# A first projection streamed by modulation pair, host-laid activations and four in-place weight slots in a two-layer diffusion trunk

## The chip, the core and the metric

The kernel runs on one core of one Trainium2 chip. The core has TensorE (PE, matmuls), VectorE (DVE), ScalarE (ACT), GpSimd (POOL) and SyncE (SP, which here only issues DMAs). Each engine works through its own list of instructions in order and meets the others only at semaphores. The metric is the device time of one execution in microseconds (us), the median of several. Where a profile is read, its own execution has a time too, and both are given.

## What is computed

A denoising step of a trunk with two layers, for 128 context and 256 latent tokens of width 1024, all in float32. Cut to what matters here:

```python
def modulate(x, g, shift, scale):
    return rms_norm(x, g) * (1 + scale) + shift
def swiglu(h, w_in, w_out):                      # w_in 1024 x 5632, w_out 2816 x 1024
    gate, up = jnp.split(h @ w_in, 2, axis=-1)
    return (jax.nn.silu(gate) * up) @ w_out
def macaron_layer(x, mod, norm_g, ffn_in, ffn_out, mixer):
    m = mod[:, :, None, :]                       # mod = silu(cond) @ w_mod + b_mod, 9 vectors of 1024
    x = x + 0.5 * m[:, 2] * swiglu(modulate(x, norm_g[0], m[:, 0], m[:, 1]), ffn_in[0], ffn_out[0])
    mixed, own_kv = mixer(modulate(x, norm_g[1], m[:, 3], m[:, 4]))
    x = x + m[:, 5] * mixed
    x = x + 0.5 * m[:, 8] * swiglu(modulate(x, norm_g[2], m[:, 6], m[:, 7]), ffn_in[1], ffn_out[1])
```

Layer 0 mixes with attention and a convolution, layer 1 with a Fourier transform and a gated unit. Context and latent tokens have conditioning vectors of their own (`c_ctx`, `c`). The outputs are the tokens of both groups, and keys and values of the context.

## The kernel before

**Stages.** Six sub-layers run one after the other, numbered s: FFN 0, the even mixer (1), FFN 2, FFN 3, the odd mixer (4), FFN 5. Tokens lie in the free dimension (384 columns: 128 context, 256 latent), channels in the partitions, eight blocks d of 128 channels. Ahead of each sub-layer stands a norm: ACT squares x, POOL and PE sum the squares, ACT and DVE make the reciprocal root, PE spreads it over the partitions, and DVE and ACT scale and shift x, block by block.

**Units.** All projection weights come in 153 units of 1 MiB (128 partitions x 2048). Every product is done by three matmuls on rounded parts: ACT copies the raw weights to `w_hi` (L528), DVE subtracts to get `w_lo` (L790), and PE computes high*high, high*low and low*high (L1185 to L1187): 48 matmuls of 384 columns a unit. An FFN has 33 units: 22 of w_in (units 0 to 21, one step each: ACT silu L557, DVE product L895, ACT `h_hi` L559, DVE `h_lo` L898), then 11 of w_out (22 to 32, the out phase). Raw, high and low parts have rings of three slots (RING = 3), and SP loads unit u as soon as the low part of unit u-3 is made (`lo_done`).

**Modulation.** Nine vectors for each of two layers are 144 row tiles of 128 outputs. The first 18 are computed at the start on PE from nine 1 MiB blocks (`w_pairs`; L1231 sums, L797 copies them out, L1241 turns them to columns). The other 126 are row tiles of 0.5 MiB (`w_rows`): for each, DVE multiplies the tile by the two conditioning rows (two L812 products, each with a sum along the row). They have a ring of three buffers: SP loads tile n after tile n-3 is used (`tile_used`). Tables say how many go with what: `TILES_BEFORE`, `TILE_LOOPS` (one tile with every step of an FFN's loop) and `TILES_OUT` (how many with each unit of the out phase). The next norm needs some of them.

**Order around the change.** In FFN s, step t of DVE splits unit t+2, makes product t and `h_lo` t, then works off its tiles. In the out phase DVE splits unit 24+j and then works off `TILES_OUT[s][j]` tiles. SP issues in one list: in the loop unit t+2, then the tile of step t; in the out phase unit 24+j, then the tiles of j. An SP instruction that waits holds all that stand behind it.

**The start.** PE transposes the conditioning rows (L1341) and x (L1350), DVE copies x out of PSUM (L947), ACT issues 13 small DMAs of vectors (L522), which PE transposes too. When all 18 tiles are done, the norm's last step runs, and FFN 0 begins with unit 0. Two conditioning rows are then loaded, and ACT applies silu (L589). **The end.** After the last residual (L852) PE transposes x back (L1573), ACT copies (L773), and SP stores (L436).

Of the kernel before, what the change touches and what calls it, by code (L numbers as in the profile page):

```python
# [26 lines left out]
P = 128  # L27
# [19 lines left out]
N_SUB = 6  # L47
# [6 lines left out]
RING = 3  # L54
MRING = 3
UNIT = 2048
# [14 lines left out]
GROUPS_FIRST = 3  # L71
LOOPS = (FT - 1) // RING
FIRST_TILES = MRING * GROUPS_FIRST * PAIR_TILES
MOD_TILES = 2 * MODT - FIRST_TILES
TILES_BEFORE = {0: 3, 2: 0, 3: 0, 5: 2}
TILE_LOOPS = {0: LOOPS, 2: LOOPS, 3: LOOPS, 5: 2}
TILES_OUT = {0: [3, 3] + [2] * 8, 2: [2] + [1] * 9, 3: [3] + [2] * 8 + [0], 5: [0] * 10}
TILE0, _t = {}, 0
for _s in (0, 2, 3, 5):
    TILE0[_s] = _t  # L80
    _t += TILES_BEFORE[_s] + MRING * TILE_LOOPS[_s] + sum(TILES_OUT[_s])
assert _t == MOD_TILES and MRING == RING
# [3 lines left out]
COND_AT = 2 * (MRING - 1)  # L86
# [70 lines left out]
def modulation_pairs(w_mod):  # L157

    n = MRING * GROUPS_FIRST
    w = w_mod[0, :, 0:n * PAIR].reshape(KT, P, n, PAIR).transpose(2, 1, 0, 3)  # L160
    return np.ascontiguousarray(w, dtype=np.float32).reshape(n, P, UNIT)
# [8 lines left out]
def build(nc, x_prompt, x_sample, cache_k, cache_v, c, c_ctx, b_mod, norm_g,  # L170
          q_norm_g, k_norm_g, conv_w, conv_b, conv_norm_g, conv_norm_b,
          sgu_norm_g, sgu_norm_b, sgu_w, sgu_b, k_ident, k_rope, k_fourier, w_units, w_pairs, w_rows,
          y_prompt, y_sample, new_cache_k, new_cache_v):
    ctx = ExitStack()
    with ctx:
# [99 lines left out]
        cols_copied = sem("cols_copied")  # L275
        const_in, cond_in, x_in = sem("const_in"), sem("cond_in"), sem("x_in")
        cond_t = sem("cond_t")
# [3 lines left out]
        rows_t, rows_c = sem("rows_t"), sem("rows_c")  # L281
        cond_ready = sem("cond_ready")
        x_t = sem("x_t")
# [9 lines left out]
        out_in, out_t, out_c, out_done = sem("out_in"), sem("out_t"), sem("out_c"), sem("out_done")  # L293
# [38 lines left out]
        def mod_rows(b):  # L332
            return m_raw[:, b, 0:D_MODEL]

        def cond_row(cnd):
            return m_raw[:, cnd, D_MODEL:UNIT]

        def row_products():
            return m_raw[:, 2, D_MODEL:UNIT]
# [3 lines left out]
        def _(sp):  # L343
            def load_unit(u, i=0):

                sp.wait_ge(lo_done, u + 1 + RING * i)
                sp.dma_start(w_raw[:, slot(u), :].unsqueeze(1),
                             w_units[bass.ds(u + i * RING, 1)].rearrange("u p n -> p u n")).then_inc(raw_in[slot(u)], 16)

            def load_pair(group, b, i=0):  # L350

                sp.wait_ge(mod_used, MRING * group + b + 1 + MRING * i)
                sp.dma_start(m_raw[:, b, :].unsqueeze(1),
                             w_pairs[bass.ds(MRING * group + b + i * MRING, 1)].rearrange("u p n -> p u n")
                             ).then_inc(mod_in[b], 16)

            def load_tile(n, i=0):

                if n >= MRING:
                    sp.wait_ge(tile_used, n - MRING + 1 + MRING * i)  # L360
                sp.dma_start(mod_rows(n % MRING).unsqueeze(1),
                             w_rows[bass.ds(n + MRING * i, 1)].rearrange("t p n -> p t n")).then_inc(tile_in[n % MRING], 16)

            def load_ffn(s):
                u0, n = UNIT0[s], TILE0[s]

                if s == 0:
# [24 lines left out]
                n += MRING * TILE_LOOPS[s]  # L392
# [1229 lines left out]
```

## Time and profile before

| what | us |
|---|---|
| median of three runs | 1502.31 (1501.9 to 1505.26) |
| the profiled execution | 1499.5 |
| its span, first to last instruction | 1497.7 |
| TensorE busy in it | 1407.8 (94%) |
| VectorE busy | 970.0 (65%) |
| mean granted TensorE clock | 0.964 |

The span is the time from the profile's first to its last instruction; 1.8 us lie around it. Busy time of PE is that of pipelined matmuls, with modelled ends. "Idle before" is the time in which an engine had nothing to do ahead of an instruction, with the work that ended it. Times of day below are from the span's start.

### The profile page before, as it was taken

The numbers are of one execution on the slowest core, as the hardware profiler recorded it, in microseconds if no ns is written. First come the engines' busy times: TensorE is split into PE (matmuls) and PEld (weight loads), VectorE is DVE, ScalarE is ACT, GpSimd is POOL, SyncE is SP. The second block draws the span as 40 slices with busy tenths as digits, with TensorE's granted clock in tenths as the row PEclk, the third lists the DMA queues.
The fourth block names the chain that finished last, engine by engine and source line by source line (L and its number), as shares of the span: only waits on it lengthen the run. The fifth ranks groups of instructions, "written<-read, shape, count | busy, mean of one in ns | idle before, by whom it ended". The sixth has DMA issues, their size and how long they took to land.

```text
span 1497.7 us, 21193 instructions
## 1 busy us (share of the span) xinstructions
PE 1407.8 (94%) x8134; PEld 1375.4 (92%) x8134; DVE 970.0 (65%) x1394; ACT 557.7 (37%) x731; POOL 122.5 (8%) x110
## 2 busy tenths in 40 slices
PE   5799999989866899999998999999989989999998
PEld 3799999989845799999998999999989989999998
DVE  2777678968998566666757666679763477444332
ACT  2433332237666443333224333332345343333221
POOL 1000000014555100000001000000021010000000
PEclk9899999989878999999998999999989999999999
DMA  8765655752200235555652555547523325433421
GB/s 325 261 231 176 203 177 200 285 182 96 86 32 29 102 133 201 188 191 174 234 181 85 197 193 185 193 149 295 219 99 134 126 85 186 137 122 130 141 84 42
DMA packets 45114, 242.96 MB, mean 162 GB/s; under 512 B 4997, under 2 KB 6889, under 8 KB 24328
## 3 DMA queue, kind: packets, MB, share of 16 engines
q1 hardware_dynamic: 44464, 241.99, 46.7%
q8 instruction: 32, 0.52, 0.1%
q10 hardware_dynamic: 600, 0.30, 0.1%
q14 instruction: 18, 0.15, 0.0%
HBM read 240.57 MB, written 1.70 MB: 162 GB/s over the span
## 4 chain that ended last, share of the span: by engine, by line
PE 83%; DVE 10%; DMA 2%; ACT 2%; issue 1%; POOL 1%; ACTq 0%; SPq 0%; DVEq 0%; POOLq 0%
PE ps L1185 27%; PE ps L1186 27%; PE ps L1187 27%; DVE conv L974 4%; DVE w_lo L790 1%; DMA conv_rows<-in_conv_w 1%; DVE n_full L876 1%; PE ps L1254 1%; DVE m_raw L812 1%; DVE smax L1039 1%; ACT w_hi L528 1%; DVE a_lo L883 0%; POOL n_acc L453 0%; DMA m_raw<-in_w_pairs 0%; PE ps L1554 0%
## 5 line engine op out<-in xcount | busy, mean ns | idle before, releaser
L1185 PE MATMUL ps<-a_hi,w_hi 128*128 128x384 f32 x1744 | 591.7, 339 | 19.1 <-DVE a_lo L883 14.0
L1186 PE MATMUL ps<-a_lo,w_hi 128*128 128x384 f32 x1744 | 588.5, 337 | 0.0
L1187 PE MATMUL ps<-a_hi,w_lo 128*128 128x384 f32 x1744 | 588.1, 337 | 0.0
L790 DVE TENSOR_TENSOR w_lo<-w_raw,w_hi 128x2048 fp32r<-128x2048 f32 x153 | 352.9, 2306 | 162.3 <-ACT w_hi L528 162.0
L528 ACT ACTIVATE w_hi<-w_raw 128x2048 fp32r<-128x2048 f32 x153 | 292.1, 1909 | 264.7 <-PE ps L1187 200.2
L1185 PEld LDWEIGHTS ps<-a_hi,w_hi 128*128 128x128 f32 x1744 | 332.1, 190 | 23.4 <-issue 10.0
L1186 PEld LDWEIGHTS ps<-a_lo,w_hi 128*128 128x128 f32 x1744 | 332.1, 190 | 0.1
L1187 PEld LDWEIGHTS ps<-a_hi,w_lo 128*128 128x128 f32 x1744 | 331.7, 190 | 0.0
L812 DVE SCALAR_TENSOR_TENSOR m_raw<-m_raw 128x1024 f32<-128x1024 f32 x252 | 296.0, 1220 | 1.0 <-ACT m_raw L589 1.0
L1187 PE MATMUL ps<-h_hi,w_lo 128*128 (+1 forms) x704 | 236.6, 336 | 0.0
L1186 PE MATMUL ps<-h_lo,w_hi 128*128 (+1 forms) x704 | 236.6, 336 | 0.0
L1185 PE MATMUL ps<-h_hi,w_hi 128*128 (+1 forms) x704 | 236.6, 336 | 0.0
L557 ACT ACTIVATE glu<-ps 128x384 f32<-128x384 f32 x88 | 43.4, 493 | 376.6 <-PE ps L1187 376.6
L895 DVE TENSOR_TENSOR glu<-glu,ps 128x384 f32<-128x384 f32 x88 | 48.7, 554 | 167.2 <-ACT glu L557 167.2
L1187 PEld LDWEIGHTS ps<-h_hi,w_lo 128*128 128x128 f32 x704 | 132.4, 188 | 0.0
L1185 PEld LDWEIGHTS ps<-h_hi,w_hi 128*128 128x128 f32 x704 | 132.4, 188 | 0.0
L1186 PEld LDWEIGHTS ps<-h_lo,w_hi 128*128 128x128 f32 x704 | 132.4, 188 | 0.0
L898 DVE TENSOR_TENSOR h_lo<-glu,h_hi 128x384 f32 (+1 forms) x88 | 49.2, 559 | 71.6 <-ACT h_hi L559 71.6
L453 POOL TENSOR_TENSOR n_acc<-n_sq 128x384 f32<-128x384 f32 x6 | 6.1, 1014 | 973.4 <-ACT n_sq L538 879.5
L559 ACT ACTIVATE h_hi<-glu 128x384 f32 (+1 forms) x88 | 46.2, 525 | 86.4 <-DVE glu L895 86.4
L473 POOL TENSOR_TENSOR conv<-conv,taps_buf 128x399 f32<-128x399 f32 x60 | 72.9, 1215 | 51.5 <-ACT taps_buf L618 45.6
L974 DVE SCALAR_TENSOR_TENSOR conv<-padded,conv_wt,conv 128x399 f32<-128x399 f32 x60 | 61.1, 1018 | 1.6
(179 smaller groups left out, 666.2 us busy)
## 6 DMA issues: line engine op xcount, KB each, us to landing
w_raw<-in_w_units SPq DMA_DIRECT2D x153, 1024.0 KB, 5.0
m_raw<-in_w_rows SPq DMA_DIRECT2D x126, 512.0 KB, 3.6
m_raw<-in_w_pairs SPq DMA_DIRECT2D x9, 1024.0 KB, 7.7
out<-x_nat SPq DMA_DIRECT2D x3, 512.0 KB, 3.1
x_nat<-in_x_sample SPq DMA_DIRECT2D x1, 1024.0 KB, 12.5
fourier<-in_k_fourier SPq DMA_DIRECT2D x1, 768.0 KB, 4.4
x_nat<-in_x_prompt SPq DMA_DIRECT2D x1, 512.0 KB, 10.7
m_raw<-in_c_ctx SPq DMA_DIRECT2D x1, 512.0 KB, 5.7
```

Of the source, the lines that this page charges most:

```text
L473: nc.gpsimd.tensor_tensor(acc, acc, taps_buf[:, n % TAP_BUFS, :], ALU.add).then_inc(tap_added, 1)
L528: nc.scalar.activation(w_hi[:, slot(u), :], w_raw[:, slot(u), :], ACT.Copy).then_inc(hi_done, 1)
L557: nc.scalar.activation(glu[:, 0, :], ps[:, 2 * b, 0:TOK], ACT.Silu).then_inc(silu_done, 1)
L559: nc.scalar.activation(h_hi[:, bass.ds(t + RING * i, 1), :], glu[:], ACT.Copy).then_inc(h_hi_done, 1)
L790: nc.vector.tensor_tensor(w_lo[:, slot(u), :], w_raw[:, slot(u), :], w_hi[:, slot(u), :].bitcast(FP32), ALU.subtract).then_inc(lo_done, 1)
L812: nc.vector.scalar_tensor_tensor(out, mod_rows(n % MRING), 1.0, cond_row(cnd), ALU.mult, ALU.mult, accum_out=mod_cols[:, bass.ds(FIRST_TIL ...
L895: nc.vector.tensor_tensor(glu[:, 0, :], glu[:, 0, :], ps[:, 2 * b + 1, 0:TOK], ALU.mult).then_inc(prod_done, 1)
L898: nc.vector.tensor_tensor(h_lo[:, bass.ds(t + RING * i, 1), :], glu[:], h_hi[:, bass.ds(t + RING * i, 1), :].bitcast(FP32), ALU.subtract). ...
L974: ins = nc.vector.scalar_tensor_tensor(conv[:, j, :], padded[:, j, k:k + CONV_N], conv_wt[:, j, k:k + 1], conv[:, j, :], ALU.mult, ALU.add)
L1185: mm(out, whi, mhi, start=start, stop=False)
L1186: mm(out, whi, mlo, start=False, stop=False)
L1187: return mm(out, wlo, mhi, start=False, stop=stop)
```

## The change

Four things, made together:

1. **The start.** The host lays out x, the conditioning vectors, all small vectors and the result in the kernel's own layout; the transposes, the copies and the 13 small DMAs go. FFN 0's first shift and scale (16 tiles) come in eight blocks, block k holding shift and scale of channel block k, all with a buffer of their own (`p_raw`). Units 0 and 1 are multiplied in k order as the pairs arrive. All squares of the first norm are summed on PE (none on POOL).
2. **The end.** Each block of x is stored after its residual, without transposes.
3. **Weight slots.** RING = 4; `w_raw` and `w_lo` share memory, so that DVE subtracts in place, and SP loads unit u only when PE is done with unit u-4 (`unit_done`).
4. **Tiles.** 128 tiles are left; the loop of an FFN has five rounds of four steps with 1, 2, 1, 2 tiles, still with three buffers, and `TILES_OUT` changes. The loop of SP loads units 3 to 22 where it loaded units 3 to 23.

```diff
-RING = 3
+RING = 4
 MRING = 3
+TRING = 3
+STEP_TILES = [1, 2, 1, 2]
-LOOPS = (FT - 1) // RING
-FIRST_TILES = MRING * GROUPS_FIRST * PAIR_TILES
+LOOPS = (FT - 2) // RING
+FIRST_TILES = KT * PAIR_TILES
-TILES_OUT = {0: [3, 3] + [2] * 8, 2: [2] + [1] * 9, 3: [3] + [2] * 8 + [0], 5: [0] * 10}
+TILES_OUT = {0: [2] * 7 + [1, 0, 0], 2: [1, 1] + [0] * 8, 3: [2] * 5 + [0] * 5, 5: [0] * 10}
...
             def load_unit(u, i=0):
-                sp.wait_ge(lo_done, u + 1 + RING * i)
+                sp.wait_ge(unit_done, u + 1 + RING * i)
...
                                 load_unit(u0 + 3 + RING * done + b, i)
                                 if with_tiles:
-                                    load_tile(n + b, i)
+                                    for t in range(STEP_TILES[b]):
+                                        load_tile(n + sum(STEP_TILES[:b]) + t, i)
...
                 for j, tiles in enumerate(TILES_OUT[s]):
-                    if j < FFN_OUT_UNITS - 2:
-                        load_unit(u0 + FT + 2 + j)
+                    load_unit(u0 + FT + 1 + j)
                     for _ in range(tiles):
                         load_tile(n)
                         n += 1
...
+            mod_sums(0)
             mod_columns(0)
+            for d in range(KT):
+                pe.wait_ge(sq_done, d + 1)
+                ins = token_sums(ps[:, 0, :], n_sq[:, d, :], d, d == KT - 1)
+            ins.then_inc(stat_done, 1)
             norm_spread(0)
+            mod_sums(1)
             mod_columns(1)
+            for k in range(KT):
+                if k + 2 < KT:
+                    mod_sums(k + 2)
+                pe.wait_ge(a_ready, k + 1)
+                for m in range(2):
+                    if k == 0:
+                        pe.wait_ge(lo_done, RING + m + 1)
+                    for h in range(2):
+                        ins = three(ps[:, 2 * m + h, 0:TOK], tile_of(w_hi, m, h * KT + k), tile_of(w_lo, m, h * KT + k),
+                                    a_hi[:, k, :], a_lo[:, k, :], k == 0, k == KT - 1)
+                    if k == KT - 1:
+                        ins.then_inc(unit_done, 1)
+                if k + 2 < KT:
+                    mod_columns(k + 2)
...
+            for d in range(KT):
+                sp.wait_ge(x_ready, KT * N_SUB + d + 1)
+                sp.dma_start(y_cols[:, d, :], x[:, d, :]).then_inc(out_done, 16)
```

On DVE the first three tiles of FFN 0, which stood ahead of step 0, now stand after step 1:

```diff
+                step(0, 0, 0, [])
                 if s == 0:
                     dve.wait_ge(silu_rows, 2)
-                for _ in range(TILES_BEFORE[s]):
-                    mod_tile(n)
-                    n += 1
-                step(0, 0, 0, None)
+                step(1, 1, 0, range(n, n + TILES_BEFORE[s]))
```

SP at the change from the loop to the out phase of FFN 0, before; the first rows are the loop's last step (unit 23, a tile), then come unit 24, three tiles, unit 25, and so on:

```order
L347 ISA [waits lo_done]
L347 DMA w_raw<-in_w_units 128x2048
L361 ISA [waits tile_used]
L361 DMA m_raw<-in_w_rows 128x1024
L386 REGISTER_ALU
L386 COMPARE_AND_BRANCH
L347 DMA w_raw<-in_w_units 128x2048 [waits lo_done]
L361 DMA m_raw<-in_w_rows 128x1024 [waits tile_used] x3
L347 DMA w_raw<-in_w_units 128x2048 [waits lo_done]
L361 DMA m_raw<-in_w_rows 128x1024 [waits tile_used] x3
```

And now; the loop's last step is unit 22 and two tiles, and the next units are 23, 24 and so on:

```order
L350 ISA [waits unit_done]
L350 DMA w_raw<-in_w_units 128x2048
L360 ISA [waits tile_used]
L360 DMA m_raw<-in_w_rows 128x1024
L360 ISA [waits tile_used]
L360 DMA m_raw<-in_w_rows 128x1024
L389 REGISTER_ALU
L389 COMPARE_AND_BRANCH
L350 DMA w_raw<-in_w_units 128x2048 [waits unit_done]
L360 DMA m_raw<-in_w_rows 128x1024 [waits tile_used] x2
L350 DMA w_raw<-in_w_units 128x2048 [waits unit_done]
L360 DMA m_raw<-in_w_rows 128x1024 [waits tile_used] x2
```

Each unit stands one step later against the tiles: the tiles of j stood behind unit 24+j, now they stand ahead of it.

PE at the start, before, from the sums of the first norm on (`n_sq`, `n_acc` are squares, `rows` small vectors):

```order
L1247 MATMUL ps<-ones,n_sq 128x1 [waits sq_done,x_ready]
L1247 MATMUL ps<-ones,n_sq 128x1 x2
L1247 MATMUL ps<-ones,n_sq 128x1 [waits sq_done]
L1247 MATMUL ps<-ones,n_sq 128x1 x2
L1247 MATMUL ps<-ones,n_acc 128x1 [waits acc_done]
L1247 MATMUL ps<-ones,n_acc 128x1 x2
```

And now, the last block's sums and what follows up to the first product of the projection:

```order
L1238 MATMUL ps<-ones,n_sq 128x1 [waits sq_done]
L1238 MATMUL ps<-ones,n_sq 128x1 x2
L1245 MATMUL ps<-n_diag,ones 128x128 [waits diag_done]
L1245 MATMUL ps<-n_diag,ones 128x128 x2
L1222 MATMUL ps<-m_raw,cond 32x256 [waits pair_in1]
L1222 MATMUL ps<-m_raw,cond 32x256 x7
L1232 MATMUL ps<-mod_pick,mod_part 128x2 [waits first_mods,part_copied]
L1232 MATMUL ps<-mod_pick,mod_part 128x2
L1222 MATMUL ps<-m_raw,cond 32x256 [waits part_copied,pair_in2]
L1222 MATMUL ps<-m_raw,cond 32x256 x7
L1175 MATMUL ps<-a_hi,w_hi 128x384 [waits lo_done,a_ready]
```

The sums stand in eight groups of three where there were three (each shows as six matmuls in the trace, in two passes), and a pair's sums stand between the products.

## Rows read from the trace of the kernel before

**Rows 1.** The page: busy time, share, instructions; then shares of the chain.

```profile
PE 1407.8 (94%) x8134; PEld 1375.4 (92%) x8134; DVE 970.0 (65%) x1394; ACT 557.7 (37%) x731; POOL 122.5 (8%) x110
PE 83%; DVE 10%; DMA 2%; ACT 2%; issue 1%; POOL 1%; ACTq 0%; SPq 0%; DVEq 0%; POOLq 0%
```

**Rows 2.** FFN 3: length, busy PE, PEld, DVE, ACT, POOL; clock, DMA share, GB/s.

```profile
811.10:1089.00 277.90, 277.55 (x1587) 277.23 (x1587) 201.57 (x280) 94.65 (x99) 4.06 (x4) 0.99 0.55 194
```

**Rows 3.** Timeline of PE, the start: start, duration, instruction, [idle before <-releaser].

```profile
7.56 1.93 PE L1231 MATMUL ps<-m_raw,cond 128*32 128x256 f32 x16 [4.03 <-DMA m_raw<-in_w_pairs]
10.05 1.93 PE L1231 MATMUL ps<-m_raw,cond 128*32 128x256 f32 x16 [0.56 <-DMA m_raw<-in_w_pairs]
...
22.90 1.50 PE L1247 MATMUL ps<-ones,n_sq 128*128 128x1 f32 x12
...
33.09 1.07 PE L1231 MATMUL ps<-m_raw,cond 128*32 128x256 f32 x16
...
41.53 1.02 PE L1241 MATMUL ps<-mod_pick,mod_part 128*128 128x6 f32 x4 [0.55 <-DVE mod_part L797]
...
67.53 0.45 PE L1185 MATMUL ps<-a_hi,w_hi 128*128 128x384 f32 x1 [1.60 <-DVE w_lo L790]
```

**Rows 4.** Timeline of PE around the norm after FFN 0.

```profile
325.39 0.34 PE L1187 MATMUL ps<-h_hi,w_lo 128*128 128x384 f32 x1
328.04 2.51 PE L1247 MATMUL ps<-ones,n_sq 128*128 128x1 f32 x12 [2.31 <-ACT n_sq L538]
...
335.24 1.65 PE L1254 MATMUL ps<-n_diag,ones 128*128 128x128 f32 x6 [1.29 <-DVE n_diag L865]
339.03 0.69 PE L1185 MATMUL ps<-a_hi,w_hi 128*128 128x384 f32 x1 [2.14 <-DVE a_lo L883]
```

**Rows 5.** Timeline of PE around the norm after FFN 2.

```profile
801.41 0.34 PE L1187 MATMUL ps<-h_hi,w_lo 128*128 128x384 f32 x1
...
811.10 0.66 PE L1185 MATMUL ps<-a_hi,w_hi 128*128 128x384 f32 x1 [2.23 <-DVE a_lo L883]
```

**Rows 6.** Timeline of DVE, two units of FFN 3's out phase.

```profile
1040.43 2.29 DVE L790 TENSOR_TENSOR w_lo<-w_raw,w_hi 128x2048 fp32r<-128x2048 f32 x1 [1.44 <-ACT w_hi L528]
1042.64 1.22 DVE L812 SCALAR_TENSOR_TENSOR m_raw<-m_raw 128x1024 f32<-128x1024 f32 x1
...
1048.75 2.29 DVE L790 TENSOR_TENSOR w_lo<-w_raw,w_hi 128x2048 fp32r<-128x2048 f32 x1 [1.45 <-ACT w_hi L528]
```

**Rows 7.** Timeline of SP there: start and duration of a unit's DMA issue.

```profile
1045.41 0.43 SPq L347 DMA_DIRECT2D w_raw<-in_w_units  x1
```

**Rows 8.** Timeline of ACT there.

```profile
1046.80 1.92 ACT L528 ACTIVATE w_hi<-w_raw 128x2048 fp32r<-128x2048 f32 x1 [6.40 <-PE ps L1187]
```

**Rows 9.** L347, issue to landing of the three units issued in 1036 to 1060.

```profile
DMA to landing us min/median/max: 5.7/5.8/5.8
```

**Rows 10.** L347, the same of the two units issued in 1008 to 1016.

```profile
DMA to landing us min/median/max: 6.6/6.8/7.0
```

**Rows 11.** Timeline of DVE, step 0 of FFN 0.

```profile
65.19 2.29 DVE L790 TENSOR_TENSOR w_lo<-w_raw,w_hi 128x2048 fp32r<-128x2048 f32 x1
67.40 0.55 DVE L895 TENSOR_TENSOR glu<-glu,ps 128x384 f32<-128x384 f32 x1
68.53 0.56 DVE L898 TENSOR_TENSOR h_lo<-glu,h_hi 128x384 fp32r<-128x384 f32 x1 [0.59 <-ACT h_hi L559]
```

**Rows 12.** Timeline of ACT ahead of it: a table load, the two conditioning rows.

```profile
54.98 1.28 ACT L589 ACT_TABLE_LOAD   x1
56.27 2.01 ACT L589 ACTIVATE m_raw<-m_raw 128x1024 f32<-128x1024 f32 x2
```

**Rows 13.** Timeline of DVE, the last residual.

```profile
1489.11 0.74 DVE L852 SCALAR_TENSOR_TENSOR x<-ps,m_gate,x 128x128 f32<-128x128 f32 x2 [0.30 <-PE ps L1187]
```

**Rows 14.** DMAs issued in the first 2 us: KB each, median us to landing.

```profile
m_raw<-in_w_pairs SPq DMA_DIRECT2D x1, 1024.0 KB, 5.5
ident<-in_k_ident SPq DMA_DIRECT2D x1, 64.0 KB, 1.9
```

More of the change, by code:

```diff
@@ L540, in norm_stats, with norm @@
                 nc.scalar.activation(stat[:, 4:4 + TT], stat[:, 0:TT], ACT.Sqrt).then_inc(root_done, 1)
-            def norm(n):
-                for d in range(KT):
+            def norm(n, d0=0, d1=KT):
+                for d in range(d0, d1):
                     for cnd, lo, hi in SEGS:
@@ L577, in _ @@
             norm_stats(0)
-            for v in range(2):
-                act.wait_ge(rows_t, v + 1)
-                nc.scalar.activation((vec_a, vec_b)[v][:], ps[:, 1 + v, 0:(A_ROWS, B_ROWS)[v]], ACT.Copy).then_inc(rows_c, 1)
-            act.wait_ge(rows_t, 3)
-            nc.scalar.activation(conv_wt[:], ps[:, 3, 0:CT * CONV_K].rearrange("p (a b) -> p a b", a=CT),
-                                 ACT.Copy).then_inc(rows_c, 1)
             split(0)
-            norm(0)
+            norm(0, 0, 1)
             split(1)
+            norm(0, 1, KT)
+            split(2)
             act.wait_ge(rows_in, 32)
@@ L770, in _ @@
             ffn(5)
-            for tt in range(TT):
-                act.wait_ge(out_t, tt + 1)
-                nc.scalar.activation(x_nat[:, tt, :].rearrange("p (a b) -> p a b", a=2), ps[:, 2 * tt:2 * tt + 2, :],
-                                     ACT.Copy).then_inc(out_c, 1)
         @block.vector
@@ L900, in step @@
                                             ALU.subtract).then_inc(h_ready, 1)
-                    if tile is not None:
+                    for tile in tiles:
                         mod_tile(tile, i)
+                step(0, 0, 0, [])
                 if s == 0:
                     dve.wait_ge(silu_rows, 2)
-                for _ in range(TILES_BEFORE[s]):
-                    mod_tile(n)
-                    n += 1
-                step(0, 0, 0, None)
+                step(1, 1, 0, range(n, n + TILES_BEFORE[s]))
+                n += TILES_BEFORE[s]
                 done = 0
@@ L990, in _ @@
             glu_mul(0)
[L991 removed]
+            dve.wait_ge(vectors_in, 48)
             split(u + 3)
@@ L1279, in step @@
                     in_unit(u0 + t, 2 * (t % RING), i)
-                first_units(u0, (0, 2), s, s != 0)
-                with pe.Fori(0, LOOPS - 1) as i:
+                if s:
+                    first_units(u0, (0, 2), s)
+                with pe.Fori(0, LOOPS) as i:
                     for b in range(RING):
                         step(2 + b, i)
-                for t in range(2 + RING * (LOOPS - 1), FT):
-                    step(t, 0)
                 def out_unit(u, t, i, first=False):
@@ L1293, in out_unit @@
                         mhi, mlo = h_hi[:, fm, :], h_lo[:, fm, :]
-                        for d in (2, 3, 4, 5, 6, 7, 0, 1) if first else range(KT):
-                            if first and h == 0 and d in (2, 4, 0):
-                                pe.wait_ge(prod_done, RING + FT * f + FT - {2: 2, 4: 1, 0: 0}[d])
+                        for d in (4, 5, 6, 7, 0, 1, 2, 3) if first else range(KT):
+                            if first and h == 0 and d % 2 == 0:
+                                pe.wait_ge(prod_done, RING + FT * f + FT - {4: 3, 6: 2, 0: 1, 2: 0}[d])
                             ins = three(ps[:, d:d + 1, 0:TOK], tile_of(w_hi, u, h * KT + d), tile_of(w_lo, u, h * KT + d),
@@ L1303, in ffn @@
                 pe.wait_ge(h_ready, 1 + FT * (f + 1))
-                with pe.Fori(0, (FFN_OUT_UNITS - 2) // RING) as i:
+                rounds = (FFN_OUT_UNITS - 2) // RING
+                with pe.Fori(0, rounds) as i:
                     for b in range(RING):
                         out_unit(u0 + FT + 1 + b, 1 + b, i)
+                for t in range(1 + RING * rounds, FFN_OUT_UNITS - 1):
+                    out_unit(u0 + FT + t, t, 0)
                 u = u0 + FFN_UNITS - 1
```

340 lines of the change are left out of this document (153 added, 187 removed).

## The prediction

> **What bounds the kernel now.** First the page, for which engine sets the end: TensorE (PE) is busy 94% of the span and carries 83% of the chain of waits, DVE 10% [rows 1]. Then busy time by stretch, to see where it is not PE: inside an FFN it is never anything else, 277.55 of 277.90 us in FFN 3 while DVE works 201.57 [rows 2]. So a gain can only come from the places where PE stands: the start, where unit 2 of FFN 0 begins at 67.53 [rows 3], the norms, and the end. In an FFN the change can only leave PE where it is or make it wait, and what decides that is how early SP may issue a load. Third, therefore, the timelines of DVE, SP and ACT in an out phase [rows 6 to 9].
>
> I keep one scale: the profiled execution of 1499.5 us, and add 2.8 at the end, by which the median is longer.
>
> **The out phase, where most of it is decided.** Call S the moment at which DVE starts a split. In FFN 3 S = 1040.43, the next split starts at 1048.75, which is PE's pace: 8.32 us a unit [rows 6]. A split takes 2.21 until the next instruction starts (1042.64), a tile is two products, 2.3 together. At 1045.41, S + 4.98, SP issues a unit [rows 7]: it had stood behind a tile that waits for the first tile of this unit's pair to be used. It lands 5.75 us later [rows 9], ACT makes its high part in 1.92, and DVE's split can follow 1.95 after ACT starts (1046.80 to 1048.75) [rows 6, 8]. So from S to the split of a unit whose load was held in this way are 4.98 + 5.75 + 1.95 = 12.7 us. Before, that was the split after the next, with 16.64 us of room. The change moves each unit one step back against the tiles: SP's list is now unit 23+j, two tiles, unit 24+j, and DVE wants 24+j in its step j. The second tile of step j waits, with three buffers, for the first tile of step j-1, and unit 24+j waits behind it. The 12.7 us now lie between one split and the next: as long as a step has two tiles behind two tiles, a unit takes **12.7 us instead of 8.32**, 4.4 lost each. PE runs two units behind the splits, but that lead is eaten before the rounds begin, as follows.
>
> FFN 3, with P the end of unit 21: product 21 comes at about P + 3.5 (PE wants it at P + 3.1, 18 matmuls into unit 22, each 8.32 / 48 = 0.173: 0.4 lost); `h_lo` and the first tile end near P + 6.9; unit 24 issued, landed and split 10.4 later, at P + 17.3, where PE wants it at P + 17.05: 0.2. Units 25 to 28 each come 12.7 after the one ahead: 4 x 4.4 = 17.6. Then the tiles are over. **FFN 3: +18.2.** FFN 2 has one tile with the first two units only, which wait for older tiles: only the 0.4 of product 21, **+0.4**. FFN 5 has none.
>
> **The start.** The first MiB lands 5.5 us after an issue at 1.9 [rows 14], the next 2.6 later (PE follows each landing [rows 3]). x (1.5 MiB) goes first: 8.7; pair 0 at 11.3. PE's sums over it take 1.93 at 1.2 GHz, the copy about 0.5 (the idle time ahead of the columns), the columns 1.02 [rows 3]: 14.8. Then the squares: 48 matmuls instead of 18 on PE. Twelve take 1.50 at the high clock [rows 3] and 2.51 at the low one [rows 4]. Which holds? Before, the sums over the first three pairs all took 1.93, and the clock rose only with the transposes of x, which go now. I take the low one: 4 x 2.51 = 10.0, to 24.8. Root and diagonal 1.3 (idle ahead of the spread), spread 1.65 [rows 4]; beside it ACT and DVE split unit 0 one after the other, 1.9 + 2.2, to 29.5. Scaling, shift and low part of block 0 follow (2.14 from spread to product before [rows 4], about 1.7 without block 1 in between), copy and columns of pair 1 (1.5), two small ones (0.3), split 1 (2.2): 35.3. PE does its first twelve products at the low clock (about 0.32 each, near double), until 38.5; columns 0.8; then five rounds at the high clock, sums 1.07 [rows 3], twelve products 2.08 and columns half of 1.02, 3.66 each: 18.3. Call the end of the last columns T: 58, half a microsecond for low clock in it. The pairs, 2.6 us apart, are ahead of this all the way. Unit 2 is split by ACT and DVE only after block 7 is scaled, T + 5.9: PE starts it at 63.9, against 67.53. **Start: -3.6.** A gain of twenty, which the stream looks like, is not in these rows: the serial chain, not the loads, is what is left.
>
> **FFN 0.** ACT loads a table and does the two rows first (3.3 [rows 12]); DVE's steps 0 and 1 (3.9 each from split to `h_lo` [rows 11]) end at T + 14.1, and only then come the three tiles. The load of unit 4 stands behind the tile that waits for the first of them: T + 16.4, issued 0.85 later, landed 5.6 later (the tile goes 0.6 ahead, not 0.4 as in [rows 9]), split 4.2 later: T + 27.1, where PE wants it at T + 22.5: **4.5**. From here DVE, SP and ACT turn in a loop of two steps: used tile, 0.85, 5.6, 1.95, then a step with two tiles (3.9 + 4.6) = 16.9 against PE's 16.64. DVE therefore never catches up; product 21 comes **5.1** after PE wants it. `h_lo` 21 and unit 24 cost 0.3 more. Units 25 to 30 cost 4.4 each: **26.4**. Together **+36.3**, a unit 32 that ends at 358 and not at 325.7.
>
> **Norm 1.** From the last product of FFN 0 to the first of the mixer PE took 13.64 us [rows 4], after FFN 2 9.69 [rows 5]; in the first case DVE was late from tiles that lay at the very end. Now the last units have none: **-4.0**.
>
> **The end.** The last residual ends at 1489.85 [rows 13], the span at 1497.7. Transposes, copies and the 512 KB stores go; a store of 192 KB is issued in 0.4 and lands within about 2.1, nearest to the 64 KB's 1.9 [rows 14]: 1492.4. **-5.3**, at worst -4.5 (a landing of 3).
>
> **Slots.** Splitting in place moves the same bytes. Loads now wait for PE's unit u-4, three units (25 us) ahead of need, against 9.9 for landing and split: no wait, also in the mixers. The extra rows of x, squares and small vectors on POOL and ACT are off the path.
>
> **Sum.** -3.6 + 36.3 - 4.0 + 0.4 + 18.2 - 5.3 = +42.0: 1541.5 on the profile's scale, **1544.3** for the median, 2.8% slower.
>
> **Rivals.** *The clock rises during the squares.* PE is busy without a break for 10 us there. Then squares and what follows go at the high clock: 4 us less in the squares, about 4 in columns, sums and first products, and all later times move up: 1536. Against it: the row of 1.93 us although PE was busy most of the time [rows 3]. For it: nothing in the rows has squares alone for so long. The Trainium skill, TensorE: Matmul & The Clock Gate, "What's actually happening", says that the throttled state is the default and activity releases it; by that rule this is the case that comes. The three 1.93 us sums before do not agree, the later rise with the transposes does. I give it 0.18.
>
> *Loads land late.* Where DVE worked without a pause, units took 6.6 to 7.0 us instead of 5.75 [rows 10]. Ten rounds at 1 us more, and eight double steps of FFN 0 at about as much, give +18: 1562. DVE is busy half of a 12.7 us round, so this is likelier in FFN 0's loop than in the rounds: 0.15.
>
> *The hold does not bite.* If the room at the start of the out phases were two splits instead of none, or SP's list ran ahead of what I read, nothing of the 54 us in the FFNs would come, and only the gains stay: 1499.5 - 3.6 - 4.0 - 5.3 + 2.8 = 1489.4, faster. It is decided by whether a round is over or under 8.32 us; landing alone is 5.75, split 4.2, so it would take an issue ahead of DVE's split. 0.07. A part of it (one FFN only, or half of the rounds), 1505 to 1530: 0.05.
>
> **How the numbers follow.** The forecast has 0.55; its own bounds (0.3 us a round, 3 in the start, 1 at the end) make 1538 to 1552. With the clock case below (1536, with the same bounds 1530) and late loads above it (to 1564) the range 1530 to 1564 leaves out the two faster ones and a few per cent above. A difference of 0.2%, 3 us, is about what a measurement of this kernel can tell from none. Faster 0.07, within it 0.01, slower 0.92.
>
> **What would show it.** In the profile after: in FFN 0's and FFN 3's out phases the splits 12.7 us apart, six and four times, PE waiting for the low part 4 us or so each time, and SP's unit issues 5 us after a split starts. Unit 4 of FFN 0 late by 4 to 5; unit 2 started near 64; twelve squares in 2.5 us. FFN 2 and 5 at 277 and 276 as before; norm 1 down to 9.7; the last store within 3 us of the last residual. Wrong it would be if splits in the out phases stay 8.32 apart, or if the mixers' units wait for their loads.

## The result, and the profile after

The changed kernel takes **1568.53 us** (median of four, 1561.49 to 1574.65), the kernel before in the same job 1502.29. The ratio is **1.0435 (95% interval 1.0384 to 1.0486)**: 66 us slower. Slower was forecast, at 1544.3 with a range up to 1564; the time lies above the range. The profiled execution took 1565.28, its span is 1563.5.

The page, answering [rows 1]: busy time, the chain, the costliest lines of the chain, and one group of the matmuls of the out phases.

```profile
PE 1436.2 (92%) x8113; PEld 1397.0 (89%) x8113; DVE 971.7 (62%) x1410; ACT 555.1 (36%) x725; POOL 113.6 (7%) x105
PE 46%; DVE 17%; DMA 16%; issue 11%; ACT 8%; SPq 1%; DVEq 1%; POOL 0%; ACTq 0%; POOLq 0%
...
L1175 PE MATMUL ps<-h_hi,w_hi 128*128 (+1 forms) x704 | 245.1, 348 | 49.1 <-DVE w_lo L767 33.3
```

PE carried 83% of the chain and now carries 46%; loads, DVE and ACT have taken its place. PE is also busy 28 us longer with fewer matmuls; 23 of them lie in FFN 0 and FFN 3, with as many matmuls as before and a lower granted clock (rows below). What it waited for (total, times, longest; `w_lo` is a unit's low part, `glu` a product):

```profile
PE ps L1175 <- DVE w_lo L767: 39.2, 14, 7.2
PE ps L1175 <- DVE glu L875: 15.6, 3, 5.6
```

The four FFNs by stretch (for FFN 0 from unit 2 on), with the columns of [rows 2]; in the kernel before PE was busy in FFN 0 for all of its 258.2 us, at a granted clock of 1.00:

```profile
62.32:366.27 303.95, 272.79 (x1488) 266.44 (x1488) 207.93 (x283) 86.75 (x86) 4.23 (x5) 0.96 0.52 188
563.41:846.80 283.39, 278.92 (x1584) 278.28 (x1584) 182.10 (x246) 95.30 (x99) 4.25 (x5) 0.98 0.49 176
854.87:1159.29 304.42, 286.18 (x1584) 282.60 (x1584) 200.32 (x278) 94.83 (x99) 4.37 (x5) 0.97 0.49 178
1282.86:1560.44 277.58, 277.58 (x1584) 277.26 (x1584) 126.80 (x149) 86.18 (x88) 0.00 (x0) 0.99 0.36 123
```

DVE in FFN 3 does what it did before (200.3 us against 201.6), but PE stands 18 us there and is busy 8.6 us longer. The whole span, each stretch from the first to the last product of its own:

| stretch | before | after | difference | forecast |
|---|---|---|---|---|
| start, to unit 2 of FFN 0 | 67.53 | 62.32 | -5.2 | -3.6 |
| FFN 0 from unit 2 | 258.20 | 303.95 | +45.8 | +36.3 |
| norm 1 | 13.30 | 8.44 | -4.9 | -4.0 |
| even mixer and its norm | 185.58 | 188.70 | +3.1 | 0 |
| FFN 2 | 277.14 | 283.39 | +6.3 | +0.4 |
| norm 3 | 9.35 | 8.07 | -1.3 | 0 |
| FFN 3 | 277.27 | 304.42 | +27.2 | +18.2 |
| odd mixer and two norms | 124.60 | 123.57 | -1.0 | 0 |
| FFN 5 | 276.10 | 277.58 | +1.5 | 0 |
| end | 8.63 | 3.06 | -5.6 | -5.3 |
| sum | 1497.7 | 1563.5 | **+65.8** | **+42.0** |

**The held rounds** are there as forecast. DVE, then SP and ACT, in FFN 3's out phase (columns as in [rows 6]):

```profile
1062.80 2.29 DVE L767 TENSOR_TENSOR w_lo<-w_raw,w_hi 128x2048 fp32r<-128x2048 f32 x1 [7.03 <-ACT w_hi L512]
...
1075.99 2.29 DVE L767 TENSOR_TENSOR w_lo<-w_raw,w_hi 128x2048 fp32r<-128x2048 f32 x1 [6.32 <-ACT w_hi L512]
...
1088.73 2.29 DVE L767 TENSOR_TENSOR w_lo<-w_raw,w_hi 128x2048 fp32r<-128x2048 f32 x1 [5.87 <-ACT w_hi L512]
```

```profile
1080.97 0.43 SPq L350 DMA_DIRECT2D w_raw<-in_w_units  x1
```

From the split at 1075.99 to the issue are 4.98 us, from there to the next split 7.76, together 12.74; [rows 6, 7] gave 12.7. DVE sits idle for 6 of them. Unit 4 of FFN 0 was late as forecast too (4.5 there, 4.27 here):

```profile
83.52 0.44 PE L1175 MATMUL ps<-a_hi,w_hi 128*128 128x384 f32 x1 [4.27 <-DVE w_lo L767]
```

**What was not forecast** stands in the loop ahead of it. DVE's splits of units 19, 21 and 23, the last of FFN 3's loop, then PE in unit 22, where it needs product 21 (the product of step 21, the last that w_in gives):

```profile
1012.87 2.29 DVE L767 TENSOR_TENSOR w_lo<-w_raw,w_hi 128x2048 fp32r<-128x2048 f32 x1 [1.88 <-ACT w_hi L512]
...
1029.96 2.29 DVE L767 TENSOR_TENSOR w_lo<-w_raw,w_hi 128x2048 fp32r<-128x2048 f32 x1 [2.02 <-ACT w_hi L512]
...
1047.04 2.29 DVE L767 TENSOR_TENSOR w_lo<-w_raw,w_hi 128x2048 fp32r<-128x2048 f32 x1 [2.01 <-ACT w_hi L512]
```

```profile
1044.02 0.34 PE L1177 MATMUL ps<-h_hi,w_lo 128*128 128x384 f32 x1
1049.86 0.69 PE L1175 MATMUL ps<-h_hi,w_hi 128*128 128x384 f32 x1 [5.50 <-DVE glu L875]
1050.34 0.53 PE L1176 MATMUL ps<-h_lo,w_hi 128*128 128x384 f32 x1
1050.66 0.53 PE L1177 MATMUL ps<-h_hi,w_lo 128*128 128x384 f32 x1
...
1053.47 0.33 PE L1177 MATMUL ps<-h_hi,w_lo 128*128 128x384 f32 x1
1053.64 0.34 PE L1175 MATMUL ps<-h_hi,w_hi 128*128 128x384 f32 x1
```

Two steps take 17.1 us (1029.96 to 1047.04) where PE takes 16.64, each second split waits 2 us for ACT and a load, and at the end of the loop PE waits 5.5 us. Behind the wait the matmuls start 0.32 apart, not 0.173, until 1053.4: some ten at the lower clock level (granted 0.50 from 1049.9 to 1053.3, 1.00 behind it), 1.7 us. FFN 2 has the same wait, without any held round behind it:

```profile
756.72 0.69 PE L1175 MATMUL ps<-h_hi,w_hi 128*128 128x384 f32 x1 [4.47 <-DVE glu L875]
```

### The profile page after: what moved, and what is told of

Same layout as the page of the kernel before. It is cut to its first block, busy times and chain, and to the rows that moved or that the text cites. A ratio compares the mean times of both kernels' runs of the same rounds, so it can differ in the third digit from the quotient of the medians.

```text
span 1563.5 us, 21066 instructions
## 1 busy us (share of the span) xinstructions
PE 1436.2 (92%) x8113; PEld 1397.0 (89%) x8113; DVE 971.7 (62%) x1410; ACT 555.1 (36%) x725; POOL 113.6 (7%) x105
## 4 chain that ended last, share of the span: by engine, by line
PE 46%; DVE 17%; DMA 16%; issue 11%; ACT 8%; SPq 1%; DVEq 1%; POOL 0%; ACTq 0%; POOLq 0%
DMA w_raw<-in_w_units 15%; PE ps L1175 14%; PE ps L1177 14%; PE ps L1176 14%; ACT w_hi L512 5%; DVE m_raw L789 5%; DVE conv L964 4%; DVE w_lo L767 3%; DVE glu L875 1%; ACT h_hi L544 1%; SPq L360 1%; PE ps L1238 1%; PE ps L1222 1%; DMA m_raw<-in_w_pairs 1%; PE ps L1245 1%
## 5 line engine op out<-in xcount | busy, mean ns | idle before, releaser
L789 DVE SCALAR_TENSOR_TENSOR m_raw<-m_raw 128x1024 f32<-128x1024 f32 x256 | 299.2, 1220 | 0.0
L1175 PE MATMUL ps<-h_hi,w_hi 128*128 (+1 forms) x704 | 245.1, 348 | 49.1 <-DVE w_lo L767 33.3
L1176 PE MATMUL ps<-h_lo,w_hi 128*128 (+1 forms) x704 | 242.8, 345 | 0.0
L1177 PE MATMUL ps<-h_hi,w_lo 128*128 (+1 forms) x704 | 242.4, 344 | 0.0
L1175 PEld LDWEIGHTS ps<-h_hi,w_hi 128*128 128x128 f32 x704 | 137.0, 195 | 54.0 <-issue 37.5
L1176 PEld LDWEIGHTS ps<-h_lo,w_hi 128*128 128x128 f32 x704 | 137.3, 195 | 0.0
L1177 PEld LDWEIGHTS ps<-h_hi,w_lo 128*128 128x128 f32 x704 | 136.9, 194 | 0.0
L826 DVE SCALAR_TENSOR_TENSOR x<-ps,m_gate,x 128x128 f32<-128x128 f32 x96 | 35.6, 413 | 63.9 <-PE ps L1177 63.9
```

Source lines behind the costliest of these rows:

```text
L789: nc.vector.scalar_tensor_tensor(out, mod_rows(n % TRING), 1.0, cond_row(cnd), ALU.mult, ALU.mult, accum_out=mod_cols[:, bass.ds(FIRST_TIL ...
L1175: mm(out, whi, mhi, start=start, stop=False)
L1176: mm(out, whi, mlo, start=False, stop=False)
L1177: return mm(out, wlo, mhi, start=False, stop=stop)
```

## The experiments

All kernels are timed against the kernel before in their own job (1502.7 to 1503.1 us there).

### SP's list put back

```diff
+                load_unit(u0 + 3)
                 done = 0
...
-                                load_unit(u0 + 3 + RING * done + b, i)
+                                load_unit(u0 + 4 + RING * done + b, i)
...
-                    load_unit(u0 + FT + 1 + j)
+                    if j < FFN_OUT_UNITS - 2:
+                        load_unit(u0 + FT + 2 + j)
```

> SP's list alone is put back: unit t+2 ahead of the tiles of step t in the loop (one more unit is loaded ahead of the loop), unit 24+j ahead of the tiles of j in the out phase. Slots, tiles, start and end are those of the changed kernel. Theory 'order' (a unit that stands behind the second tile of a step waits for the first tile of the step before): all waits of TensorE inside the FFNs go. From unit 2 on FFN 0 takes 258 us instead of 304, FFN 2 277 instead of 283, FFN 3 277 instead of 304; together -79, 1486 us for the profiled execution, 1% faster than the kernel before. Rival 'tiles' (two tiles a step are too much work for DVE beside a split): splits stay 12.7 apart, 1565. Rival 'slots' (loads wait for TensorE to release unit u-4, not for tiles): 1565 as well. Rival 'late loads' (landings of 7 to 9 us carry half of it): about 1525.

Measured: **1486.15 us** (1483.77 to 1487.51), ratio 0.9885 (0.9867 to 0.9903). FFN 0 from unit 2, and FFN 3:

```profile
61.00:320.06 259.06, 258.48 (x1488) 257.83 (x1488) 207.45 (x283) 86.84 (x87) 4.24 (x5) 1.00 0.63 220
...
802.72:1080.38 277.66, 277.66 (x1584) 277.35 (x1584) 200.17 (x278) 94.63 (x99) 4.25 (x5) 0.99 0.56 197
```

PE is busy all of 277.66 us with the same DVE work as in the changed kernel. So neither the work of the tiles nor the slots cost anything: where each unit stands in SP's list made the 82 us between the two kernels (1568.53 and 1486.15). Loads landed no earlier here: of the 107 units 3 to 109 (up to FFN 3), 35 took over 6.3 us from issue to landing, against 17 in the changed kernel. They now have two splits of room.

### Six tile buffers, SP's list as in the change

```diff
-MRING = 3
-TRING = 3
+MRING = 5
+TRING = 6
...
```

The lines left out keep three tiles ahead of FFN 0's loop and shift the count by which SP waits ahead of a tile.

> SP's list as in the changed kernel, but six tile buffers instead of three (two more 1 MiB buffers beside the tiles; three pairs instead of five have a buffer of their own at the start, and the conditioning rows are loaded after the fifth pair is used). Theory 'order': the second tile of a step now waits for a tile of three steps earlier, so nothing is held: as with the order put back, 1486 us, FFN 0 from unit 2 on 258, FFN 3 277. Rivals 'tiles' and 'slots': no change, 1565. If the order alone gains and this does not, the transfer's place in the queue matters and not the wait.

Measured: **1485.35 us** (1484.33 to 1486.83), ratio 0.9878 (0.9861 to 0.9894). FFN 3:

```profile
804.59:1081.69 277.10, 277.10 (x1584) 276.78 (x1584) 200.07 (x278) 94.63 (x99) 4.25 (x5) 0.99 0.54 195
```

The same gain with the order untouched. The place of the transfer in the queue is nothing in itself; what costs is that SP stands at a tile's wait with the unit behind it.

### One half of the order at a time

Only the loops put back (in the out phase the tiles of j, then unit 24+j):

> Only the loops' order is put back; in the out phases the tiles of j still stand ahead of unit 24+j. Theory 'order': unit 4 of FFN 0 and product 21 in FFN 0, 2 and 3 are on time, FFN 2 takes 277; the rounds of the out phases stay at 12.7 us, six times in FFN 0 (258 + 27 = 285 from unit 2 on) and four times in FFN 3 (277 + 18 = 295): 1565 - 19 - 6 - 9 = 1531. Rival 'late loads': the loops' order matters little, 1560.

Measured: **1533.2 us** (1532.26 to 1535.35). Only the out phases put back (unit 24+j, then the tiles of j; loops as in the change):

> Only the out phases' order is put back; the loops stay. Theory 'order': no rounds of 12.7 us, but unit 4 of FFN 0 late by 4 to 6, double steps of 17.1 us instead of 16.64 in three loops, product 21 late by about 5 in each and some 1.6 us of low clock behind each such wait: FFN 0 275 from unit 2 on, FFN 2 283, FFN 3 285: 1565 - 29 - 19 = 1517. Rival 'late loads': 1545.

Measured: **1524.35 us** (1520.81 to 1527.34). Windows of FFN 0 and 3 with the loops put back, then of FFN 0, 2 and 3 with the out phases put back, and the waits of PE in the latter:

```profile
61.60:349.60 288.00, 267.00 (x1488) 264.48 (x1488) 207.53 (x283) 86.83 (x86) 4.24 (x5) 0.97 0.56 198
832.50:1130.58 298.08, 284.11 (x1584) 282.26 (x1584) 200.30 (x278) 94.71 (x99) 4.37 (x5) 0.97 0.52 183
```

```profile
63.46:340.31 276.85, 263.94 (x1488) 262.39 (x1488) 207.73 (x283) 86.81 (x86) 4.24 (x5) 0.97 0.57 207
535.78:823.40 287.62, 281.40 (x1584) 279.84 (x1584) 181.97 (x246) 95.20 (x99) 4.36 (x5) 0.98 0.49 174
831.92:1117.04 285.12, 280.87 (x1584) 280.23 (x1584) 200.23 (x278) 95.42 (x99) 4.37 (x5) 0.98 0.52 190
```

```profile
PE ps L1177 <- DVE glu L877: 15.3, 3, 5.7
...
PE ps L1177 <- DVE w_lo L769: 9.2, 4, 6.8
```

With the loops in order FFN 0 takes 29 us more than with both in order and FFN 3 20, all of it in the out phases, and product 21 is never late. With the out phases in order the three late products 21 are all there. Against 1486.15 the out phases' order costs 47 us and the loops' 38, together 85 where both at once cost 82. FFN 2 is 4.6 us longer than expected: a load of 8.1 us (unit 19) delays PE by 1.2 ahead of unit 22, product 21 comes 5.75 us late and not about 5, and the ten units behind it run at 8.48 us each instead of 8.32, 1.6 us. The executions of this kernel are 6.5 us apart, those of the changed kernel 13; those of the kernels without a held loop 1.5 to 4.5.

### The tiles spread in FFN 3

```diff
-3: [2] * 5 + [0] * 5
+3: [1] * 10
```

> The changed kernel with one table row changed: FFN 3's ten tiles of the out phase stand one with each unit instead of two with each of the first five. SP's order and three buffers stay. Theory 'order': one tile behind one tile waits for a tile of three steps earlier, so nothing is held in FFN 3's out phase; the loop with two tiles in every second step stays, and with it product 21 about 5 late and 1.7 of low clock behind it. FFN 3 takes 285 us instead of 304, FFN 0 stays at 304 from unit 2 on: 1565 - 19 = 1546. The norm after it may be up to 2 us later from a tile with the last unit. Rival 'tiles' (the work of the tiles itself): as many tiles, no change, 1565.

Measured: **1547.93 us** (1546.02 to 1556.02). FFN 3 and its only long wait:

```profile
856.27:1140.48 284.21, 278.80 (x1584) 278.16 (x1584) 200.53 (x278) 95.43 (x99) 4.25 (x5) 0.98 0.54 190
```

```profile
1049.69 0.69 PE L1175 MATMUL ps<-h_hi,w_hi 128*128 128x384 f32 x1 [5.41 <-DVE glu L875]
```

As many tiles, no round of 12.7 us, 20 us back (304.42 to 284.21). The norm behind it took 8.5 us as before: the tile with the last unit was free.

### The order alone, in the kernel before

```diff
-                                load_unit(u0 + 3 + RING * done + b, i)
                                 if with_tiles:
                                     load_tile(n + b, i)
+                                load_unit(u0 + 3 + RING * done + b, i)
...
-                    if j < FFN_OUT_UNITS - 2:
-                        load_unit(u0 + FT + 2 + j)
                     for _ in range(tiles):
                         load_tile(n)
                         n += 1
+                    if j < FFN_OUT_UNITS - 2:
+                        load_unit(u0 + FT + 2 + j)
```

> The kernel before with SP's order alone changed: the tile of step t stands ahead of unit t+2 in the loops, the tiles of j ahead of unit 24+j in the out phases (old start, old end, three slots, old tables). Theory 'order': the loops, one tile a step, lose nothing. In the out phases, where the last tile of a step waits for a tile of the step before: first tile of two: rounds of 12.7; last of three behind three: 2.2 + 6.9 + 8.55 = 17.65; second of two behind three 15.35; first unit behind three tiles 14.75. FFN 0: 6.4 + 9.3 + 7.0 + 6 x 4.4 = 49; FFN 2: 0; FFN 3: 6.4 + 7.0 + 7 x 4.4 = 44; 1502 + 93 = 1595, down to 1587 if each FFN has 4 us of lead. If slots or the changed loops are needed for the loss: 1502 to 1510.

Measured: **1601.3 us** (1600.45 to 1601.94), ratio 1.0652 (1.0635 to 1.067). The out phase of FFN 0, FFN 2 whole, the out phase of FFN 3, and four splits of the first:

```profile
235.14:372.98 137.84, 104.60 (x529) 101.70 (x528) 69.84 (x95) 20.05 (x12) 0.00 (x0) 0.89 0.43 160
585.00:861.68 276.68, 276.68 (x1584) 276.37 (x1584) 182.82 (x246) 94.42 (x99) 3.45 (x4) 0.99 0.49 181
1056.37:1186.42 130.05, 103.11 (x529) 100.27 (x528) 73.03 (x104) 25.40 (x19) 0.98 (x1) 0.91 0.46 171
```

```profile
249.24 2.29 DVE L790 TENSOR_TENSOR w_lo<-w_raw,w_hi 128x2048 fp32r<-128x2048 f32 x1 [9.18 <-ACT w_hi L528]
268.20 2.29 DVE L790 TENSOR_TENSOR w_lo<-w_raw,w_hi 128x2048 fp32r<-128x2048 f32 x1 [9.79 <-ACT w_hi L528]
283.92 2.29 DVE L790 TENSOR_TENSOR w_lo<-w_raw,w_hi 128x2048 fp32r<-128x2048 f32 x1 [6.56 <-ACT w_hi L528]
296.71 2.29 DVE L790 TENSOR_TENSOR w_lo<-w_raw,w_hi 128x2048 fp32r<-128x2048 f32 x1 [5.92 <-ACT w_hi L528]
```

Rounds of 18.96, 15.72 and 12.79 us where 17.65, 15.35 and 12.7 were worked out. The order alone makes the kernel before 98 us slower; with one tile a step (loops, FFN 2) it costs nothing. The out phases lose 46 and 38 us (91.7 without), 8.5 less than expected in sum, near the 4 us of lead for each FFN that the expectation allowed. The norms behind them lose 10 and 4, which was not in the expectation. In FFN 0 DVE works off its last tiles until 379.9, 6.9 us behind PE's last product (372.98), and only then starts the residual, which the norm waits for; in the kernel before it started the residual at 322.8, ahead of PE's last product (325.7).

### The start: clock and squares

Twenty matmuls of ones ahead of the first pair, on the kernel with the list put back:

```diff
+            pe.wait_ge(setup, 2)
+            for _ in range(20):
+                mm(ps[:, 3, 0:P], ones[:], ones[:], start=True, stop=True)
             pe.wait_ge(cond_ready, 2)
```

> The kernel with SP's list put back, and twenty matmuls of ones by ones (128 columns, results not used) on TensorE ahead of the first pair, where it waits for the first 11 us. Question: does the granted clock rise, and do one-column squares and 32-row sums keep it? If both: 48 square matmuls 5.3 us instead of 10.4, sums of a pair 1.07 instead of 1.94, unit 2 of FFN 0 starts at 53 instead of 61, 1486 - 8 = 1478. If small matmuls let it fall again, the squares take over 9 us and the whole gain is under 2: 1485.

Measured: **1485.42 us** (1481.86 to 1486.39), no gain that can be told; unit 2 starts at 63.3, where it starts at 61.0 to 63.5 in the changed kernel and the runs above with its start. Timeline of PE (20 matmuls of ones show as 40):

```profile
1.26 6.31 PE L1333 MATMUL ps<-ones 128*128 128x128 f32 x40 [1.26 <-POOL ones L445]
11.28 1.85 PE L1224 MATMUL ps<-m_raw,cond 128*32 128x256 f32 x16 [3.71 <-DMA m_raw<-in_w_pairs]
...
14.67 10.38 PE L1240 MATMUL ps<-ones,n_sq 128*128 128x1 f32 x48
```

The ones did raise the clock (7 matmuls a us until 4 us, 10 to 11 from 5 on), but 0.3 us into the sums, behind the pause of 3.7 us, it was granted at 0.50 again. So 36 of them, without a pause:

> As with twenty matmuls of ones, but 36 of them (72 in the trace), so that TensorE has no pause of 3.7 us ahead of the first pair: twenty ended at 7.6, sixteen more at about 0.28 each end near 12, within a microsecond of the pair's landing. With the pause the clock was back at its lower level with the first sums. If the pause let it fall, the sums now take 1.07 and, if one-column matmuls hold it, the 48 squares 5.3: unit 2 of FFN 0 near 54, 1478. If the squares themselves let it fall, they start fast and end slow (8 to 10 us) and what follows stays slow: 1484 to 1486.

Measured: **1481.16 us** (1480.55 to 1482.41), ratio 0.9855 (0.984 to 0.987). Sums and squares, then two stretches inside the squares (PE alone: length, busy and count, clock, DMA share, GB/s):

```profile
12.00 1.07 PE L1224 MATMUL ps<-m_raw,cond 128*32 128x256 f32 x16
...
14.22 8.05 PE L1240 MATMUL ps<-ones,n_sq 128*128 128x1 f32 x48
```

```profile
14.20:16.70 2.50, 2.50 (x25) 1.00 1.00 423
16.90:22.20 5.30, 5.30 (x26) 0.50 1.00 417
```

In the squares it is the second of the two outcomes: 25 matmuls in 2.50 us (23 of them squares, the others columns), then 26 in 5.30, at a granted clock of 1.00 and 0.50 (2.4 and 1.2 GHz), with no idle time between them. The clock fell while one-column matmuls ran back to back. A pause of 0.71 us lies ahead of the columns before them, and no run leaves it out; but in the changed kernel a pause of 1.23 us ahead of unit 2 was followed by matmuls at the high level. The time came out below the 1484 to 1486 of that outcome: unit 2 starts at 58.8, 2.2 earlier than with the list put back (61.0), and what else the 5 us hold is not in the start.

The other way is to have fewer of them. Squares of the first norm summed on POOL, as in the kernel before (five adds, 18 matmuls instead of 48):

> The kernel with SP's list put back, and the first norm's squares summed as in the kernel before: five adds on POOL, 18 matmuls instead of 48 on TensorE. At 10.4 us for 48 the 18 take 3.9; POOL's five adds at 1.02 end at about 15, when TensorE comes from the first columns. Unit 2 of FFN 0 starts at 54.7 instead of 61.2: 1486 - 6.5 = 1479.5. Rival (POOL's adds are late or the pairs bound the rounds instead): under 2 us gained.

Measured: **1478.58 us** (1477.55 to 1480.87), ratio 0.9839 (0.9823 to 0.9856). The time is the one expected, the start is not: unit 2 of FFN 0 starts at 57.19, not at 54.7, 3.8 us earlier than with the list put back. Of the 6.0 us between the two profiled executions 2.3 lie in the even mixer's stretch (188.5 and 186.2), which the edit leaves as it was and which scatters by 3 us among these runs. Both together:

> SP's list put back, squares on POOL, and the 36 matmuls of ones ahead of the first pair. The 18 square matmuls come right behind the columns. If the clock is held over them: squares 2.2 instead of 4.1, sums and columns of pairs 0 to 2 half of 8, first products 1.5 less: 1478.6 - 6 = 1472.5. If it falls in the squares or in the idle time between them and the spread: 1 to 2 us less than without the ones, 1477.

Measured: **1475.54 us** (1475.06 to 1478.31), ratio **0.9828 (0.9815 to 0.9841)**, the fastest of all. Squares and spread:

```profile
14.61 1.48 PE L1241 MATMUL ps<-ones,n_sq 128*128 128x1 f32 x12
15.95 0.81 PE L1241 MATMUL ps<-ones,n_acc 128*128 128x1 f32 x6
18.05 1.65 PE L1248 MATMUL ps<-n_diag,ones 128*128 128x128 f32 x6 [1.29 <-DVE n_diag L842]
20.41 1.94 PE L1225 MATMUL ps<-m_raw,cond 128*32 128x256 f32 x16 [0.70 <-DMA m_raw<-in_w_pairs]
```

The squares take 2.2 us, but the spread, after 1.29 us idle, and the sums behind it are at the lower level again, and PE waits 0.70 for pair 1: here, for the first time, the stream itself is near. Unit 2 starts at 53.8, 3.4 us earlier than without the ones, and 3.0 us of the 6 that a held clock was to give are seen in the time.

## Why the prediction was right and where it was wrong

**Right: the mechanism, and its size in the rounds.** The unit behind a waiting tile, 12.7 us a round, six and four rounds: the traces show it, and it goes with the order (82 us), with more buffers, and in FFN 3 with one tile a step, and it comes into the kernel before with the order alone. With the loops in order, out phases are 29.0 and 22.0 us too long where the rounds were counted at 26.4 and 17.6; the rest is for the most part a load of 7.4 us in FFN 0 and one of 6.9 in FFN 3, and the low clock behind the last round (1.7 and 3.0 us). That the rounds are held by the order and not by slots or late loads was the forecast's view, at 0.55.

**Right: the start and the end.** Squares at the lower clock (10.38 us forecast as 10.0), five rounds of 3.66 (3.64 measured), unit 2 at 62.3 for 63.9. It came 1.6 earlier largely because three of the first twelve products ran at the low clock, and not all of them. (Twelve at 0.32 from 35.3 on would end at 39.1; the forecast's sum has 38.5.) The timeline:

```profile
15.04 10.38 PE L1238 MATMUL ps<-ones,n_sq 128*128 128x1 f32 x48
...
62.32 0.44 PE L1175 MATMUL ps<-a_hi,w_hi 128*128 128x384 f32 x1 [1.23 <-DVE w_lo L767]
```

The rival of a rising clock falls, by this row and by the runs with ones: the 48 squares don't keep a clock that they are given. What the Trainium skill says (TensorE: Matmul & The Clock Gate, "What's actually happening"), that activity releases the throttled state, holds here for the 72 matmuls of ones, and not for the 48 squares, which are as dense. The ones ran at 7 a us until 6 us and at 10 from 8 us on. The span ended 2.3 us after the last residual (1561.2), norm 1 fell to 8.4 us.

**Wrong: the loops of FFN 2 and 3, and a charge left out in FFN 0.** The step that failed is "FFN 3, with P the end of unit 21: product 21 comes at about P + 3.5", and with it, for FFN 2, "only the 0.4 of product 21". In FFN 3 product 21 came at P + 8.9 (1049.86 against a P of 1041.0). The double step of 16.9 us had been worked out for FFN 0 alone, as if it came from that FFN's late unit 4. It is a property of the loop's order: in all three loops a unit stands behind the second tile of a double step, the turn takes 17.05 to 17.1 us against PE's 16.64, and each late landing adds itself, since DVE never makes it up: behind landings of 7.2 us at unit 11, that turn of FFN 2 and FFN 3 took 18.9. In FFN 2 and 3 this uses up DVE's lead, and product 21 comes 4.5 and 5.5 us late. In FFN 0 the forecast had DVE late from unit 4 on and said that it never catches up, but did not charge PE for walking at DVE's pace: 9 double steps at 0.41 are 3.7, measured 3.6 (from the start of unit 4 to that of unit 22 155.0 us passed for 149.8, less 1.7 for the clock). That the two agree is partly luck: DVE's nine turns took 157.2 us, 7.4 too many, 3.1 of it from the late landings of units 7 and 9 (7.3 and 6.8 us), and the slower matmuls behind unit 4 had given DVE some room.

**Left out: the clock behind a wait.** After the wait for unit 4 48 matmuls took 10.2 us instead of 8.5, and after the waits for product 21 the rest of unit 22 took 1.5 to 1.8 more than at the high level. Ahead of and inside the rounds this is hidden, as DVE sets their pace there; behind unit 4 of FFN 0 and behind product 21 of FFN 2 it is paid, 1.7 and 1.5 us.

The 24 us that were missing are these: 1.4 at unit 4 of FFN 0, 3.6 in its loop, 4.3 in its out phase (3.0 of it one landing of 8.8 us), 5.9 in FFN 2 and 9.0 in FFN 3. There the low part of unit 24, which waits for step 21, is ready 24.0 us after P (1062.80 + 2.21) and not 17.3: 6.7 of the 9.0. The others (mixers, norms, FFN 5, start, end) sum to -0.5. The even mixer's +3.1 can't be told from scatter: with the mixer of the kernel before, in the run with its order changed, the same stretch took 188.5, and in the other kernels with the new slots 186.2 to 189.1. The slots cost nothing: with the list put back, the only wait of PE for a low part over 1 us outside the mixers is the 1.23 us ahead of unit 2.

**The rival "loads land late"** was priced nearest to the result (1562). It is not what made the loss: with the list put back, more loads took over 6.3 us (35 against 17) and cost nothing. But on top of the order it has a share that the forecast kept out of its sum. From the split of unit 7 to that of unit 23, eight turns, DVE took 138.2, 138.8 and 139.9 us in FFN 0, 2 and 3; eight undisturbed turns of 17.07 are 136.6, and PE's 133.1. So 3.5 us in each loop are the turn itself, and 1.6, 2.3 and 3.3 are late landings. Without these, product 21 would have come about 2.2 us late in FFN 2 and in FFN 3, by this estimate, not 4.5 and 5.5. With the 3.0 of one landing in FFN 0's out phase and 1.2 of unit 24's in FFN 3 (6.96 us for 5.75), some 11 of the 24 us are late landings in this one execution. They count only where a unit has no room, and in the kernels with held loops the executions spread by 6.5 to 13 us. That the spread comes from them is likely and was not tested.

**The rest of the forecast's range.** The bounds took 0.3 us a round and gave nothing to FFN 2 and to the clock after a wait. The rows for both were there: that in every loop a unit stands behind the second tile of a double step is read from the change itself, and a wait of over 4 us in an FFN appeared in no row of before, so its clock should have had a bound from the norm, where [rows 4] show first matmuls of 0.69 us for 0.34.

## What to carry to other kernels

In a queue that works in order, ask of every load what stands ahead of it and may wait. A load that is late by its own need must not stand behind one that waits for a consumer; put it one step ahead, or give the other stream so many buffers that it does not wait. Where a loop's turn through engine, queue and landing is longer than the bound engine's by even 2%, charge it in every loop that has that order, add it up over the rounds, and remember that it can make up nothing that lands late.

## What the runs showed of the hardware

- TensorE's granted clock fell from 1.00 to 0.50 within a gapless row of one-column matmuls (25 matmuls in 2.50 us, then 26 in 5.30). The row of 128-column matmuls of ones (10 a us from 8 to 12 us) and the FFNs' rows of 384 columns (277.66 us without a gap in FFN 3, clock 0.99) were as dense and did not lose it.
- Idle time of 1.3 us (ahead of the spread) behind such squares, or of 3.7 us behind 128-column matmuls, was followed by matmuls at the lower level; after waits of 1.6 to 2.8 us in the out phases it was so in some cases (48 matmuls in 10.2 us) and not in others (8.6 us). What decides between these is open.
- The clock column reads 1.00 in the changed kernel's start, where 48 squares took 10.38 us, and 0.50 for the same pace in the run with twenty ones. In that stretch the durations tell the level, and the column does not.
- Behind FFN 3's last held round four units ran at 8.48 us instead of 8.32 without a wait between them, at a granted clock of 1.00. With the out phases put back it was all ten units behind product 21, in FFN 2 and in FFN 3, and none in FFN 0. The cause is open.
